# SSM products on two or four tiles of TensorE, fewer and larger moves, and the residual's scaling placed behind the attention

## The reference

```
xn = rmsnorm(h); q, k, v, u, gates = split(xn @ w_in)
attn = stick_breaking_attention(rmsnorm(q), rmsnorm(k), v)     # 4 heads of 64, strictly causal
y    = s5_ssm(u)                                               # 32 groups of 16 channels, 64 complex states
g    = gelu(y);  ssm = g * sigmoid(g @ w_glu + b_glu)
h = h + (sigmoid(gate_a) * (attn @ w_attn_proj) + sigmoid(gate_s) * (ssm @ w_ssm_proj)) @ w_o
h = h + (silu(conv_g) * conv_v) @ w_down                       # conv = causal 3-tap of rmsnorm(h) @ w_up
```

## Time and profile before

| | |
|---|---|
| median of 3 runs | 713.1 us (712.81 to 713.95) |
| the profiled execution | 712.44 us, of which the span from first to last instruction is 710.7 us |
| PE busy | 702.5 us, 99% of the span |
| DVE, ACT, POOL busy | 58%, 45%, 26% |
| granted TensorE clock | 1.000 of full speed |

### The profile page before, as it was taken

The page is one execution under the profiler, slowest core; times in us unless marked ns, Lnnn a source line. Parts: engine busy times, 40 slices in busy tenths (PEclk is TensorE's granted clock), DMA queues, the critical chain, the costliest instruction groups (busy, mean ns, idle before and its releaser), DMA issues.

```text
span 710.7 us, 13993 instructions
## 1 busy us (share of the span) xinstructions
PE 702.5 (99%) x5552; PEld 668.8 (94%) x5552; DVE 415.4 (58%) x557; ACT 319.7 (45%) x474; POOL 187.6 (26%) x215
## 2 busy tenths in 40 slices
PE   8999999999999999999999999999999999999998
PEld 7899899989999999999999999999999998888887
DVE  5764488867787756545765666666666662222221
ACT  4754343558888654435443444443343442211220
POOL 7899999940000022232011010101011010000000
PEclk9999999999999999999999999999999999999999
DMA  8163444545211233333333332323333343333331
GB/s 230 56 201 81 95 126 97 106 96 164 60 33 60 66 90 112 89 90 92 89 99 100 95 89 89 89 89 89 89 98 97 105 121 89 97 96 96 96 97 45
DMA packets 140520, 69.25 MB, mean 97 GB/s; under 512 B 24067, under 2 KB 138471, under 8 KB 140479
## 3 DMA queue, kind: packets, MB, share of 16 engines
q1 hardware_dynamic: 140319, 68.65, 35.0%
q10 hardware_dynamic: 160, 0.02, 0.0%
HBM read 63.19 MB, written 4.28 MB: 95 GB/s over the span
## 4 chain that ended last, share of the span: by engine, by line
PE 90%; DVE 3%; ACT 3%; SPq 1%; issue 1%; DMA 1%; POOL 0%; DVEq 0%; ACTq 0%
PE ps L1803 81%; PE ps L1987 1%; PE ps L2045 1%; PE ps L1854 1%; PE ps L1952 1%; PE ps L2012 1%; ACT xh L982 1%; SPq L626 1%; DMA xtok<-in_x_dram 1%; SPq L533 1%; ACT hi L913 1%; PE ps L1863 1%; PE ps L1921 1%; PE ps L1904 0%; PE ps L1947 0%
## 5 line engine op out<-in xcount | busy, mean ns | idle before, releaser
L1296 DVE TENSOR_TENSOR lo<-raw,hi 128x1024 fp32r<-128x1024 f32 (+2 forms) x102 | 136.5, 1339 | 152.6 <-ACT hi L913 152.3
L1803 PE MATMUL ps<-xh,hi 128*128 128x264 f32 (+1 forms) x1088 | 219.6, 283 | 0.1
L1803 PE MATMUL ps<-xl,hi 128*128 128x264 f32 (+1 forms) x1088 | 218.7, 282 | 0.0
L913 ACT ACTIVATE hi<-raw 128x1024 fp32r<-128x1024 f32 (+2 forms) x102 | 111.5, 1093 | 237.1 <-PE ps L1803 232.3
L1803 PE MATMUL ps<-xh,lo 128*128 128x264 f32 (+1 forms) x1088 | 217.9, 282 | 0.0
L1803 PEld LDWEIGHTS ps<-xh,hi 128*128 128x128 f32 x1088 | 167.2, 189 | 1.7 <-issue 0.8
L1803 PEld LDWEIGHTS ps<-xl,hi 128*128 128x128 f32 x1088 | 166.7, 188 | 0.0
L1803 PEld LDWEIGHTS ps<-xh,lo 128*128 128x128 f32 x1088 | 166.7, 188 | 0.0
L896 POOL TENSOR_TENSOR cv<-cv 128x512 f32<-128x512 f32 x22 | 28.4, 1289 | 226.7 <-DVE cv L1755 226.7
L1803 PE MATMUL ps<-ah,hi 128*128 128x512 f32 (+1 forms) x198 | 74.3, 375 | 0.0
L1803 PE MATMUL ps<-al,hi 128*128 128x512 f32 (+1 forms) x198 | 73.1, 369 | 0.0
(11 more groups left out here) (291 smaller groups left out, 966.1 us busy)
## 6 DMA issues: line engine op xcount, KB each, us to landing
raw<-in_w_up_dram SPq DMA_DIRECT2D x88, 256.0 KB, 3.1
raw<-in_w_in_dram SPq DMA_DIRECT2D x52, 256.0 KB, 3.4
raw<-in_w_down_dram SPq DMA_DIRECT2D x16, 384.0 KB, 3.3
raw<-in_w_down_dram SPq DMA_DIRECT2D x16, 320.0 KB, 4.0
raw<-in_w_o_dram SPq DMA_DIRECT2D x16, 256.0 KB, 2.9
xtok<-in_x_dram SPq DMA_DIRECT2D x4, 512.0 KB, 5.7
raw<-in_w_ssm_proj_dram SPq DMA_DIRECT2D x8, 256.0 KB, 2.9
out_dram<-yt SPq DMA_DIRECT2D x7, 256.0 KB, 2.4
```

Source lines behind the costliest of these rows:

```text
L913: act.activation(hi[slot][:, 0:n * P], raw[slot][:, 0:n * P], ACT.Copy)\
L1296: dve.tensor_tensor(lo[slot][:, 0:n * P], raw[slot][:, 0:n * P], hi[slot][:, 0:n * P].bitcast(F32), ALU.subtract)\
L1803: ins = pe.matmul(o, weights[w], acts(a, c), start=start and i == 0, stop=stop and i == 2)
```

## The change

- `prep` on PE: the products with `bpair` alternate between output partitions 0 to 47 and 64 to 111, two groups of states at once.
- `readout` on PE: each product of L1952 (64 rows by 128 columns) becomes two of 64 rows by 64 columns. Order: both column halves of the even group (rows 0 to 63), then both of the odd group (rows 64 to 127).
- `output_map`'s real part for rounds 0, 1 and 2 is DVE's, in units 6, 7 and 8; round 3 is wholly POOL's.
- u is read for two rounds at once (2 x 8 DMAs in place of 4 x 8), into a buffer for all four rounds. y is written by one DMA a round into a DRAM buffer of another layout, and read back by 8 DMAs of 264-byte pieces.
- `turn_v` in three pieces (2, 4, 4 transposes) on bank 7 in place of two (5, 5) on banks 4 and 5.
- The first two heads' splits (`head`) stand in units 15 and 16 ahead of the last readout's ACT work.
- `scores`: a bank's mask products come first, then its q and k products.
- The eight multiplications of `hT` on POOL wait for the last head's values (`av_ps`).

Cut to its core:

```diff
-MOVES = {2: [("u_write", 0)], 3: [("u_write", 1)], 4: [("u_write", 2), ("u_read", 0)],
-         5: [("u_write", 3), ("u_read", 1)],
+MOVES = {2: [("u_write", 0)], 3: [("u_write", 1)], 4: [("u_write", 2)],
+         5: [("u_read", 0), ("u_write", 3)], 6: [("u_read", 1)],
...
             def y_write(r):
                 sp.wait_ge(yg_set, r + 1)
-                dst = y_dram[r * P:(r + 1) * P].rearrange("(g h) j c -> j h g c", h=GH)
-                for j in range(T8):
-                    sp.dma_start(dst[j], yg[GH * j:GH * (j + 1)]).then_inc(y_out[r], 16)
+                sp.dma_start(y_dram[r].rearrange("j h g c -> (j h) (g c)"),
+                             yg[:].rearrange("p g c -> p (g c)")).then_inc(y_out[r], 16)
...
-                sp.dma_start(yT[:], y_dram.rearrange("(r p) j c -> p r j c", p=P)).then_inc(y_in, 16)
+                for g in range(2 * RP):
+                    sp.dma_start(yT[GH * g:GH * (g + 1)].rearrange("p r j c -> p (r j) c"),
+                                 y_dram[:, :, :, g].rearrange("r j h c -> h (r j) c"))\
+                        .then_inc(y_in, 16)
...
             pool.wait_ge(rb_in, 16)
+            pool.wait_ge(av_ps, HEADS)
             for k in range(KD):
                 pool.tensor_tensor(hT[:, k, :], hT[:, k, :], rb[:], ALU.mult).then_inc(h_raw, 1)
...
-                for i in range(RP):
+                pe.wait_ge(h_dve, min(r + 1, HOUTS))
+                for k in range(RP // 2):
                     for c in range(2):
-                        ins = pe.matmul(ps[0:3 * GH, 6, i * P:(i + 1) * P],
-                                        bpair[:, c, r * RP + i, :],
-                                        hout[r % HOUTS][:, c, i, 0:T8, :].rearrange("p i h -> p (i h)"),
-                                        start=c == 0, stop=c == 1)
+                        for half in range(2):
+                            i = 2 * k + half
+                            p0 = ST * half
+                            ins = pe.matmul(ps[p0:p0 + 3 * GH, 6, k * P:(k + 1) * P],
+                                            bpair[:, c, r * RP + i, :],
+                                            hout[r % HOUTS][:, c, i, 0:T8, :]
+                                            .rearrange("p i h -> p (i h)"),
+                                            start=c == 0, stop=c == 1)
...
                 for c in range(2):
                     for g in range(2 * RP):
                         part = slice(ST * (g % 2), ST * (g % 2) + ST)
-                        ins = pe.matmul(group_out(g), hout[r % HOUTS][part, c, g // 2, 1:T8 + 1, :]
-                                        .rearrange("p i h -> p (i h)"),
-                                        xst[part, c, g // 2, :], start=False, stop=c == 1,
-                                        skip_group_check=True)
+                        maps = hout[r % HOUTS][part, c, g // 2, 1:T8 + 1, :]\
+                            .rearrange("p i h -> p (i h)")
+                        for half in range(2):
+                            mine = slice(ST * half, ST * half + ST)
+                            ins = pe.matmul(group_out(g)[mine], maps[:, mine],
+                                            xst[part, c, g // 2, :], start=False, stop=c == 1,
+                                            skip_group_check=True)
```

More of the change, by code:

```diff
@@ L102 @@
          3: [("turns", 0)], 4: [("columns", 1), ("turns", 1)],
[L103 to L108, removed]
+         5: [("square", 0)], 6: [("square", 1), ("out_map", 0)],
+         7: [("square", 2), ("out_map", 1)], 8: [("square", 3), ("out_map", 2), ("prep", 0)],
+         9: [("state", 0), ("norms", 0)],
+         10: [("prep", 1), ("turn_v", 0)], 11: [("readout", 0), ("state", 1)],
+         12: [("prep", 2), ("turn_v", 1)] + [("scale", i) for i in range(4)], 13: [("readout", 1), ("state", 2)],
+         14: [("prep", 3), ("turn_v", 2)], 15: [("readout", 2), ("state", 3), ("head", 0)],
+         16: [("head", 1), ("readout", 3)],
          17: [("scores", 0)], 18: [("suffix", 0)], 19: [("values", 0), ("scores", 1)],
@@ L127 @@
 NORM_ROWS = (0, 32)
-TURN_BANK = (4, 4)
+TURN_BANK = 7
 HOUTS = 3
@@ L289, in hybrid_trunk @@
         lal = alloc(heads, "lal", [P, SUM_COLS], F32R)
+        ql2 = [alloc(heads, f"ql2{i}", [P, LL], F32R) for i in range(2)]
         k2 = [alloc(heads, f"k2{i}", [P, L], F32R) for i in range(2)]
@@ L369, in hybrid_trunk @@
         u_out = [sem(f"u_out{i}") for i in range(ROUNDS)]
-        u_in = [sem(f"u_in{i}") for i in range(ROUNDS)]
+        u_in = [sem(f"u_in{i}") for i in range(2)]
         y_out = [sem(f"y_out{i}") for i in range(ROUNDS)]
@@ L616, in u_write, with u_read @@
                 sp.dma_start(u_dram[r * P:(r + 1) * P], uy[:, r % 2]).then_inc(u_out[r], 16)
[L618 to L623, removed]
+            def u_read(two):
+                rounds = slice(2 * two, 2 * two + 2)
+                for u in u_out[rounds]:
+                    sp.wait_ge(u, 16)
+                src = u_dram.rearrange("(r g h) j c -> j h r g c", h=GH, r=ROUNDS)
                 for j in range(T8):
                     p0 = GH * (T8 - 1 - j)
-                    sp.dma_start(uc[p0:p0 + GH, r % 2], src[j]).then_inc(u_in[r], 16)
+                    sp.dma_start(uc[p0:p0 + GH, rounds].rearrange("p r g c -> p (r g) c"),
+                                 src[j, :, rounds].rearrange("h r g c -> h (r g) c"))\
+                        .then_inc(u_in[two], 16)
             def toep_move(r):
@@ L1418, in out_map @@
                     dve.wait_ge(y_ps, r - HOUTS + 1)
+                if r == 0:
+                    dve.wait_ge(pw_set, 1)
+                    for u in u_out:
+                        dve.wait_ge(u, 16)
                 map_part(dve, link, r, 0, mod_flat)
@@ L1663, in _ @@
                      "norms": norms, "scale": scale, "prep": prep, "state": state,
-                     "readout": readout,
+                     "head": head,
                      "scores": scores, "suffix": suffix, "values": values, "gelu": gelu,
@@ L2058, in run @@
                     pe.wait_ge(masks_set, 4)
-                bank = {"turn_v": TURN_BANK}.get(name, (0,) * 4)[i]
-                if bank == 4 or name in ("prep", "state", "scores") or (name, i) == ("columns", 0):
+                if name in ("prep", "state", "scores") or (name, i) == ("columns", 0):
                     for s_, n in used45 if name != "scores" else ():
```

144 lines of the change are left out of this document (74 added, 70 removed).

## The result

The changed kernel takes 718.0 us (median of ten executions, 715.3 to 718.8) against 713.1 us for the kernel before, measured beside it: a ratio of 1.0064, with a 95% interval of 1.0054 to 1.0074. The forecast was 711.9 us, with 706 to 715 as its range, so the time lies outside. The profiled execution took 717.9 us, with a span of 716.2 us (before: 712.4 and 710.7).

What follows compares the result with a forecast made beforehand. PE, busy 99% of the span, was taken to bound the kernel. Savings of 6.15 us on PE and a cost of 4.9 us from DVE and POOL gave -1.25 us: 713.1 to 711.9 us, range 706 to 715.

Steps and rivals of the forecast that it cites:

- What costs nothing: Map moves, DMAs, copies, turn_v: covered by slack; POOL's last input map ends before PE's last prep, a miss up to 1.5 us.
- (a): PE's prep, four rounds: bpair products alternating column tiles save 0.8 us a round, -3.2 us in all.
- (b): PE's readout, four rounds: 64 xst records on four tiles in place of 32, -1.0 us in all.
- (c): Last readout: PE's 1.2 us wait for xst goes as DVE's last state step runs without POOL beside it, -1.1 us.
- (d): First head's suffix on PE: operands' splits made earlier, so it no longer waits for them, -0.45 us.
- (e): PE's mask products put together ahead of a bank, and the 0.17 us gap at the last prep: -0.4 us.
- (f): Behind the attention: POOL's hT multiplications collide with DVE's GLU chain, PE waits ahead of unit 28 and for sl, +4.9 us.
- the strict replay by turns: GLU chain behind the attention: POOL and DVE alternate whole instructions, last sl at 253.8, PE loses 6.1 us.
- packing brings nothing: Rival on the bpair and xst stretches: no saving in prep, readout slower, 716.9 us; chance 0.20.
- Rival 3: Readout's four tiles run at once and POOL/DVE turns cost 6.1 us: 710.6 us, a variant inside the main case's range.

Runs made afterwards that it cites:

- experiment 2: Changed kernel with the real part of the last output map back on DVE (step 12), shared with POOL: 712.8 us, 0.9993 of the kernel before.
- experiment 6: Kernel before with only the packing (bpair on two column tiles, 64 xst products on four, ACT's fitting copies): 713.2 us, ratio 1.0001.
- experiment 5: Changed kernel with 30 unused identity transposes on PE ahead of its wait for POOL's last input map: 715.1 us, 1.0023 of the kernel before.
- experiment 1: Changed kernel with POOL's eight hT multiplications back at their old place, no wait for the last head: 711.3 us, 0.9971 of the kernel before.
- experiment 10: experiment 9's kernel with the packing taken out (bpair on one tile, 32 xst records, ACT's two copies): 712.8 us, 0.9998 of the kernel before.
- experiment 9: Changed kernel, last output map shared behind the scalings, five hT multiplications after DVE's last sl tile, three between POOL's sums: 707.4 us, 0.9929 of kernel before.
- experiment 4: Kernel before with only the eight hT multiplications held back until the last head's values: 719.7 us, ratio 1.0104.
- experiment 7: experiment 2's kernel with the hT multiplications released by DVE's last sl tile instead of the last head: 708.1 us, 0.9926 of the kernel before.
- experiment 11: Changed kernel with POOL's hT multiplications by constant 1 instead of tile rb, residual's normalisation left out: 712.7 us, 0.9996 of the kernel before.

## Why the prediction was wrong

**The step that failed** is in "What costs nothing": POOL's last input map "should end near 128, and PE, 3.6 us earlier by then, gets there at 129.2. A miss would cost up to 1.5 us." PE came at 128.9; POOL ended at 132.6. I had counted two maps of 5 us given away against one taken. The timelines of POOL before and after show what that left out:

```profile
80.63 1.42 POOL L494 TENSOR_TENSOR gates<-gates,pt 128x576 f32<-128x576 f32 x1
82.23 0.65 POOL L518 TENSOR_TENSOR g_in<-pw,bb 128x256 f32<-128x256 f32 x1 [0.18 <-POOL gates L494]
```
```profile
76.67 0.69 POOL L524 TENSOR_TENSOR g_in<-pw,bb 128x256 f32<-128x256 f32 x1 [3.15 <-PE ps L1924]
...
107.72 0.71 POOL L498 TENSOR_TENSOR gates<-pw,ct 128x288 f32<-128x288 f32 x1 [0.18 <-POOL g_in L529]
...
120.72 0.88 POOL L524 TENSOR_TENSOR g_in<-pw,bb 128x256 f32<-128x256 f32 x1 [0.18 <-POOL gates L500]
...
131.52 1.07 POOL L529 TENSOR_TENSOR g_in<-g_in,pt 128x256 f32<-128x256 f32 x1
```

The second input map may not start before PE has read the first. With the maps ahead of it gone, POOL stood for 3.15 us, and the chain behind began 5.6 us earlier (82.23 to 76.67), not 10. The part taken back is no 5 us either: both parts of the last output map take 13.0 us (107.72 to 120.72), 6.5 each, where the shortest of these instructions in the two traces (0.70, 0.77 and 0.81 us, with 0.08 between them) would make an estimated 5.0. DVE works beside them. 6.5 more, less 0.5 that the rest of the chain took less, against a start 5.6 earlier leaves the end 0.4 us later than before, at 131.52 + 1.07 = 132.59 us, while PE came 3.9 us earlier. The earlier trace rows had said that PE's arrival and POOL's end were 0.7 us apart; whatever shortens PE ahead of that point has to shorten POOL too. Experiments 2 and 6 show it from both sides. Cost: 3.7 us, and 1.4 to 1.5 of clock. With this step put right, experiment 2 measured 712.8 us.

**What the forecast did not have at all** is the clock: no term asked what a wait does to the work behind it. It added 1.4 us to the one wait and 1.7 us to the others. The first is shown by experiment 5; the second is read from the windows, and no run took it away by itself.

**(a)** Right: 1.01 us a round, inside the forecast 1.0 to 1.15. **(b)** Too small by 2.4 us: four tiles overlap nearly fully, 17 ns a record where a quarter of the 57 ns of a record alone would be 14, and the term is -3.4, about the end of -3.5 for four tiles at once. The Trainium skill, "TensorE: Matmul & The Clock Gate", section "Wait — 56ns, not 53.3ns?", has a floor of about 25 ns between the starts of two matmuls however small they are; the 64 records in 1.09 us, which go to four tiles in turn, stay below it, and the measurement decides. **(c)** Right in its mechanism, -1.2, of which 0.4 came back as a wait for `toep`, which I had put at a tenth. **(d)** Failed: the first suffix takes the same 3.06 us, now behind a wait of 0.3 us; the wait names `awl`, the softmax's low part, so the earlier splits of keys and queries did not bring it forward. In experiments 1 and 10, which have the same splits, the first suffix shows no wait, and its first and last records start 2.6 us apart in place of 2.9. The runs differ in ACT ahead of it, which waits for the weights of its next copy: 3.15 us in the changed kernel (3.05 in experiment 9), 2.2 in those two.

```profile
155.76 1.06 ACT L925 ACTIVATE hi<-raw 128x1024 fp32r<-128x1024 f32 x1 [3.15 <-DMA raw<-in_w_in_dram]
```

That this wait is the cause was not tested. **(e)** -0.1 in place of -0.4.

**(f)** Right in its place and nearly in its size: the strict replay by turns had DVE's second `sl` pair end at 253.8, less the 1.8 us by which the head ended earlier 252.0, and it ended at 251.46. PE lost 5.5 us there, 5.1 of it in the two waits, between the 6.1 of the replay and the 4.9 that I took. That 4.9 was so close to the 5.1 is partly luck, since the turn taken off was a guess. Experiment 1 removed the two waits, experiment 4 made them alone. The picture behind the replay is only half right. The Trainium skill, "SBUF — State Buffer", section "SBUF: two separate sides", says that DVE with two SBUF inputs and a GpSimd instruction that reads SBUF exclude each other for the whole instruction. That operands in PSUM are spared agrees with experiment 7; that the whole instruction is waited for does not agree with experiment 11.

Of the rivals, "packing brings nothing" came nearest in its time (716.9), but by another mechanism than it named: the stretches did shorten, and the time was lost in waits behind them. Rival 3 had the four tiles right and the turns to within 0.6 us, and gave 710.6 us; it too lacked the wait for POOL and the clock. The profiled span came out 6.7 us above the sum of the terms (+5.5 for -1.25): the wait for POOL 3.7, the clock 3.1, (d) 1.0 with the late first scores, (f)'s slower pace 0.6, start-up 0.4, (c) and (e) 0.6, against 2.4 too little counted for (b) and 0.3 for (a).

## What to carry to other kernels

When a change makes the bounding engine faster, list each engine that delivers to it just in time, and move its start and its own waits, not only its amount of work: here all of 6.9 us saved on PE vanished until POOL's maps and the multiplications beside DVE were moved too. A wait of some microseconds can cost more than its length: where the slower clock followed, it added 1.4 to 1.7 us. Work that can go anywhere belongs where the engine beside it reads from PSUM or stands still, and in pieces that never stand ahead of something that is waited for.

## What was not expected of the hardware

Four tiles of 64 x 64 with 66 columns start every 17 ns (1.09 us for 64). Waits of 3.88 us, and of 2.20 and 2.93 us within 7 us, were followed by about 3 us in which the granted clock was at or near 0.5 of 2.4 GHz, the 1.2 GHz level; the wait of 1.2 us in the kernel before was not (1.00). Length alone did not decide it: a wait of 2.2 us was followed by the lower level in experiment 4 and by full clock in the changed kernel, and a wait of 3.0 us in experiment 6 by full clock. A multiplication by a constant on POOL took 1.52 us at the shortest where one by a tile took 1.29, and held DVE up far less.
